# An LRU in-projection in three passes on split values, with its heads written out, and filler matmuls in TensorE's waits

## The reference

```
proj = x @ w_in                      # (288, 2048) @ (2048, 4096)
gate_br, u = split(proj, 2)
uc = causal depthwise conv of u (4 taps) + bias
r  = sigmoid(uc @ w_a + b_a);  ig = sigmoid(uc @ w_x + b_x)     # per head, 8 heads of 256
a  = exp(-8 * r * softplus(-lambda));  b = sqrt(1 - a^2) * ig * uc
h  = scan over time of  h = a*h + b
out = (h * gelu(gate_br)) @ w_out
x  = layer_norm(alpha * x + out)
x  = layer_norm(alpha * x + moe(x))  # 4 groups x 4 experts, routed, 2 experts per token
```

## Time and profile before

| | |
|---|---|
| median of 3 runs | 1817.91 us (1817.19 to 1818.08) |
| profiled execution, its own time | 1817.13 us |
| its span, first to last instruction | 1815.1 us |
| mean granted TensorE clock | 0.953 |
| PE busy | 1659.0 us (91%), 7572 instructions |
| PEld / DVE / ACT busy | 1200.1 / 1313.6 / 1070.6 us |
| LRU heads, first in-projection product to the end of the last head's line 841 | 26.70 to 306.70 us |
| out-projection | 324.02 to 427.46 us |
| time in the chain of waits on line 830 / 841 | 14% / 2% of the span |

### The profile page before, as it was taken

The page is one execution under the profiler, slowest core; times in us unless marked ns, Lnnn a source line. Parts: engine busy times, 40 slices in busy tenths (PEclk is TensorE's granted clock), DMA queues, the critical chain, the costliest instruction groups (busy, mean ns, idle before and its releaser), DMA issues.

```text
span 1815.1 us, 20866 instructions
## 1 busy us (share of the span) xinstructions
PE 1659.0 (91%) x7572; PEld 1200.1 (66%) x7572; DVE 1313.6 (72%) x1658; ACT 1070.6 (59%) x1223; POOL 45.0 (2%) x34
## 2 busy tenths in 40 slices
PE   6999997897799999999999958869999999999995
PEld 5777775895576666766666636556665675665664
DVE  1333334654678998998998856567899899899887
ACT  1132224333657787787787842355877777777774
POOL 0000000000000000000000000000001001000100
PEclk9999999899889999999999977888999999999998
DMA  9443436252479999999999962266998999998990
GB/s 285 141 153 113 150 127 208 93 177 101 156 280 325 388 366 329 400 357 344 378 360 341 372 220 93 98 226 249 369 368 333 339 389 332 344 385 330 337 381 14
DMA packets 146405, 487.90 MB, mean 269 GB/s; under 512 B 5324, under 2 KB 59276, under 8 KB 126892
## 3 DMA queue, kind: packets, MB, share of 16 engines
q1 hardware_dynamic: 141328, 463.75, 69.7%
q0 software_dynamic: 2464, 13.37, 2.5%
q10 hardware_dynamic: 2522, 9.59, 1.6%
HBM read 476.15 MB, written 14.47 MB: 270 GB/s over the span
## 4 chain that ended last, share of the span: by engine, by line
PE 77%; DVE 12%; issue 4%; ACT 3%; DMA 2%; ACTq 1%; DVEq 0%; POOL 0%; POOLq 0%
PE ps L997 17%; PE ps L999 16%; PE ps L998 16%; PE ps L830 14%; DVE ring_lo L1415 6%; PE ps L859 2%; PE ps L861 2%; PE ps L860 2%; PE ps L1042 2%; PE ps L841 2%; PE ps L915 1%; DVE xtok L1373 1%; DVE zstat L1377 1%; DMA xtok<-x_rows,src_now 1%; PE ps L923 1%
## 5 line engine op out<-in xcount | busy, mean ns | idle before, releaser
L1415 DVE TENSOR_TENSOR ring_lo<-ring,whi 128x1024 fp32r<-128x1024 f32 x768 | 922.1, 1221 | 115.7 <-ACT whi L703 108.3
L703 ACT ACTIVATE whi<-ring 128x1024 fp32r<-128x1024 f32 x768 | 806.2, 1060 | 256.2 <-PE ps L999 249.2
L997 PE MATMUL ps<-whi,operands 128*96 128x512 f32 x1536 | 625.0, 407 | 35.3 <-issue 17.6
L999 PE MATMUL ps<-ring_lo,operands 128*96 128x512 f32 x1536 | 610.7, 398 | 0.0
L998 PE MATMUL ps<-whi,operands 128*96 128x512 f32 x1536 | 608.9, 396 | 0.0
L997 PEld LDWEIGHTS ps<-whi,operands 128*96 128x96 f32 x1536 | 250.4, 163 | 169.4 <-DVE ring_lo L1415 40.4
L999 PEld LDWEIGHTS ps<-ring_lo,operands 128*96 128x96 f32 x1536 | 251.1, 163 | 112.4 <-issue 0.2
L998 PEld LDWEIGHTS ps<-whi,operands 128*96 128x96 f32 x1536 | 252.7, 165 | 100.1 <-issue 0.8
L830 PE MATMUL ps<-xT,ring 128*128 128x288 f32 x1024 | 249.7, 406 | 0.7 <-ACT mark L571 0.7
L830 PEld LDWEIGHTS ps<-xT,ring 128*128 128x128 f32 x1024 | 194.4, 190 | 54.6 <-ACT mark L571 0.8
L859 PE MATMUL ps<-operands,whi 128*128 128x288 f32 x256 | 76.7, 300 | 17.3 <-DVE ylo L1205 17.3
(11 more groups left out here) (263 smaller groups left out, 1039.9 us busy)
## 6 DMA issues: line engine op xcount, KB each, us to landing
ring<-in_moe_w_gate_up SPq DMA_DIRECT2D x128, 2048.0 KB, 9.1
ring<-in_moe_w_down SPq DMA_DIRECT2D x64, 2048.0 KB, 9.9
ring<-in_lru_w_in SPq DMA_DIRECT2D x16, 2048.0 KB, 9.6
ring<-in_lru_w_out SPq DMA_DIRECT2D x8, 2048.0 KB, 8.5
x_rows<-xtok ACTq DMA_DIRECT2D x4, 1024.0 KB, 3.9
ring<-in_pool_w SPq DMA_DIRECT2D x4, 1024.0 KB, 6.4
xtok<-in_x_prompt SPq DMA_DIRECT2D x2, 1024.0 KB, 9.2
ring<-in_lru_w_a SPq DMA_DIRECT2D x8, 256.0 KB, 5.4
```

Source lines behind the costliest of these rows:

```text
L703: eng.activation(whi[:, i % NPART, :], ring_at(n)[:, at * PART:(at + 1) * PART], ACT.Copy)\
L997: mm(o, hi, whi[:, i % NPART, cols], start=start, stop=False)
L999: last = mm(o, hi, lo_at(base + i // PARTS_CHUNK, i % PARTS_CHUNK)[:, cols], start=False, stop=stop)
L1415: TT_(lo_at(n, at), ring_at(n)[:, at * PART:(at + 1) * PART], whi[:, i % NPART, :].bitcast(F32), ALU.subtract).then_inc(lo_ready, 1)
```

## The change

The in-projection works on split values as the out-projection does. `x` is split into `yhi` and into 16 blocks of `xlo`, which lie in the unused part of the two ring slots that hold `w_a` and `w_x`. The eight heads are written out on SP, ACT, PE and DVE instead of looped. The first four parts of the next head (for the last head, of the out-projection) are split inside the head before. `SelfOrder` counts per head (14 links instead of 28 per turn). `chunks_done` now counts once per head, so its later thresholds are smaller. In addition PE runs 12, 8 and 10 matmuls whose results nobody reads, at three kinds of place: 12 at the start of each mixture of experts, 8 before the first window of each, and 10 at the end of layer 0.

```diff
+PARTS_HEAD = 2 * PARTS_CHUNK
+PARTS_LRU = HEADS * PARTS_HEAD
+XLO_SPLIT = 10
...
+        def xlo_block(k):
+            slot, at = (SLOT0 + 2) % NSLOT if k < XLO_SPLIT else (SLOT0 + 5) % NSLOT, 1024 + (k % XLO_SPLIT) * T
+            return ring_lo[:, slot, at:at + T]
...
```

On SP:

```diff
+            def lru_slot_free(n):
+                if n % 3 < 2:
+                    eng.wait_ge(parts_used, NPART + (n // 3) * PARTS_HEAD + (n % 3 + 1) * PARTS_CHUNK)
+                else:
+                    eng.wait_ge(chunks_done, n // 3 + 1)
...
             for i in range(N_OUT):
                 n = C_OUT + i
                 if i < NSLOT:
-                    eng.wait_ge(chunks_done, n - NSLOT + 1)
+                    lru_slot_free(n - NSLOT)
+                    if i == 2:
+                        eng.wait_ge(parts_used, NPART + PARTS_LRU)
...
```

On ACT:

```diff
+            def high_part(p):
+                n, at = ((p // PARTS_HEAD) * 3 + (p % PARTS_HEAD) // PARTS_CHUNK if p < PARTS_LRU else
+                         C_OUT + (p - PARTS_LRU) // PARTS_CHUNK), p % PARTS_CHUNK
+                if at == 0:
+                    eng.wait_ge(ring_ready[slot_of(n)], ready_at(n))
+                eng.wait_ge(parts_used, p + 1)
+                eng.activation(whi[:, p % NPART, :], ring_at(n)[:, at * PART:(at + 1) * PART], ACT.Copy)\
+                   .then_inc(hi_ready, 1)
+
+            eng.wait_ge(tr_act[0], 6)
+            eng.wait_ge(tr_dve[0], 6)
+            for q in range(4):
+                eng.activation(yhi[:, 4 * q:4 * q + 4, :], xT[:, 4 * q:4 * q + 4, :], ACT.Copy).then_inc(xs_hi, 1)
+                high_part(q)
             eng.wait_ge(derived, 1)
             eng.activation(sp[1][:, :], sp[0][:, :], ACT.Exp, scale=-1.0).then_inc(lam_exp, 1)
             eng.activation(mark[0:1, 30:31], tiny[0:1, 0:1], ACT.Copy).then_inc(u_copied, 2)
...
+            for h in range(HEADS):
+                for p in range(4, 8):
+                    high_part(h * PARTS_HEAD + p)
+                eng.wait_ge(parts_used, NPART + h * PARTS_HEAD + PARTS_CHUNK)
+...
+                for p in range(8, 12):
+                    high_part(h * PARTS_HEAD + p)
+                eng.wait_ge(parts_used, NPART + (h + 1) * PARTS_HEAD)
+...
-            for part in range(PARTS_OUT):
...
+            eng.wait_ge(head_done, HEADS + 1)
+            for k in range(KD):
+                eng.activation(yhi[:, k, :], yT[:, k, :], ACT.Copy).then_inc(yhi_ready, 1)
+            for p in range(PARTS_LRU + NPART, PARTS_LRU + PARTS_OUT):
+                high_part(p)
...
```

On PE:

```diff
+            for h in range(HEADS):
+                for j in range(2):
+                    if j == 1:
+                        eng.wait_ge(gelu_done, h + 1)
+                    else:
+                        eng.wait_ge(u_copied, 2 * h + 2)
+                    for q in range(PARTS_CHUNK):
+                        p = h * PARTS_HEAD + j * PARTS_CHUNK + q
+                        if h == 0 and j == 0:
+                            eng.wait_ge(xs_lo, q + 1)
+                        eng.wait_ge(lo_ready, p + 1)
+                        for k in range(4 * q, 4 * q + 4):
+                            for b in range(2):
...
+                                mm(o, hi, yhi[:, k, :], start=(k == 0), stop=False)
+                                mm(o, hi, xlo_block(k), start=False, stop=False)
+                                last = mm(o, lo, yhi[:, k, :], start=False, stop=(k == KD - 1))
+                        last.then_inc(parts_used, 1)
+...
+            def stay_awake(n):
+                for _ in range(n):
+                    mm(ps[:, 2, 0:T], onesd[:, :], prmT[:, 0:T], start=True, stop=True)
+
             def moe(l):
+                stay_awake(12)
...
                 eng.wait_ge(tr_act[1 + l], 12)
+                if l == 0:
+                    eng.wait_ge(cstT_ready, 1)
+                stay_awake(8)
                 eng.wait_ge(rows_in[l], 16)
...
                 if l == 0:
                     pe_extra.append(eng.snap(n_win - NG))
+                    eng.wait_ge(z_done[0], eng.snap(n_win * 4 + 4))
+                    eng.wait_ge(rows_out[0], eng.snap(n_win * 16))
+                    stay_awake(10)
                     eng.wait_ge(back_in, 48)
...
```

On DVE:

```diff
+            def low_part(p):
+...
+                eng.wait_ge(hi_ready, p + 1)
+                TT_(lo_at(n, at), ring_at(n)[:, at * PART:(at + 1) * PART],
+                    whi[:, p % NPART, :].bitcast(F32), ALU.subtract).then_inc(lo_ready, 1)
+
+            for q in range(4):
+                eng.wait_ge(xs_hi, q + 1)
+                for k in range(4 * q, 4 * q + 4):
+                    ins = TT_(xlo_block(k), xT[:, k, :], yhi[:, k, :].bitcast(F32), ALU.subtract)
+                ins.then_inc(xs_lo, 1)
+                low_part(q)
...
+            for h in range(HEADS):
+                for p in range(4 if h == 0 else 5, 8):
+                    low_part(h * PARTS_HEAD + p)
+...
+                for p in range(8, 12):
+                    low_part(h * PARTS_HEAD + p)
+...
+                if h < HEADS - 1:
+                    low_part(h * PARTS_HEAD + 12)
+...
-            for part in range(PARTS_OUT):
-                n, at = C_OUT + part // PARTS_CHUNK, part % PARTS_CHUNK
-                if part == NPART:
...
+            for k in range(KD):
+                eng.wait_ge(yhi_ready, k + 1)
+                TT_(ylo[:, k, :], yT[:, k, :], yhi[:, k, :].bitcast(F32), ALU.subtract).then_inc(ylo_ready, 1)
+            for part in range(NPART, PARTS_OUT):
```

More of the change, by code:

```diff
@@ L90, in parts_base @@
 def parts_base(l):
[L92 removed]
+    return PARTS_LRU + PARTS_OUT + l * NG * PARTS_WIN
 def slot_of(n):
@@ new lines, in _ @@
+            for h in range(HEADS):
+                for j in range(2):
+                    n = 3 * h + j
+                    if j == 1:
[8 more added lines that the diff above has]
+                        for k in range(4 * q, 4 * q + 4):
+                            for b in range(2):
+                                at = (k % 4) * 256 + b * 128
+                                hi, lo = whi[:, p % NPART, at:at + 128], lo_at(n, q)[:, at:at + 128]
+                                o = ps[:, 2 * j + b, 0:T]
+                                mm(o, hi, yhi[:, k, :], start=(k == 0), stop=False)
+                                mm(o, hi, xlo_block(k), start=False, stop=False)
+                                last = mm(o, lo, yhi[:, k, :], start=False, stop=(k == KD - 1))
+                        last.then_inc(parts_used, 1)
+                n = 3 * h + 2
+                eng.wait_ge(ring_ready[slot_of(n)], ready_at(n))
+                eng.wait_ge(uc_ready, h + 1)
+                eng.wait_ge(ri_read, h + 1)
+                wv = ring_at(n)[:, 0:1024].rearrange("p (a k j) -> p a k j", a=2, k=2)
+                for a in range(2):
+                    for b in range(2):
+                        for k in range(2):
+                            last = mm(ps[:, 4 + 2 * a + b, 0:TG], wv[:, a, k, b * 128:(b + 1) * 128], UC[:, k, :],
+                                      start=(k == 0), stop=(k == 1))
+                last.then_inc(chunks_done, 1)
@@ L849, in _ @@
                 for q in range(PARTS_CHUNK):
-                    part = i * PARTS_CHUNK + q
+                    part = PARTS_LRU + i * PARTS_CHUNK + q
                     if i == 0:
@@ L1198, in _ @@
                 TS_(slot_iota[:, w * W:(w + 1) * W], iota_f[:, 0:W], float(w * W), None, ALU.add)
[L1199 to L1205 removed]
+            for k in range(KD):
+                eng.wait_ge(yhi_ready, k + 1)
+                TT_(ylo[:, k, :], yT[:, k, :], yhi[:, k, :].bitcast(F32), ALU.subtract).then_inc(ylo_ready, 1)
+            for part in range(NPART, PARTS_OUT):
                 if part >= PARTS_CHUNK + NPART and (part - NPART) % PARTS_CHUNK == 0:
                     out_add((part - NPART) // PARTS_CHUNK - 1)
[L1208 to L1210 removed]
+                low_part(PARTS_LRU + part)
             for i in range((PARTS_OUT - 1 - NPART) // PARTS_CHUNK, N_OUT):
```

223 lines of the change are left out of this document (81 added, 142 removed).

## The result

| | before | after |
|---|---|---|
| median of 4 runs each, on one chip | 1817.55 us (1814.25 to 1818.08) | 1775.12 us (1773.60 to 1777.10) |
| ratio of the runs | | 0.9771, 95% interval 0.9760 to 0.9782 |
| profiled execution, its own time / its span | 1817.13 / 1815.1 us | 1773.60 / 1771.8 us |
| mean granted TensorE clock | 0.953 | 0.961 |
| first in-projection product | 26.70 us | 32.92 us |

What follows compares the result with a forecast made beforehand. PE alone was taken to bound the LRU, ACT and DVE hidden. Passes -44.4, start +9.8, end -4.2 give -38.8; with fillers -3.7, -42.5 us: 1775.4 us against the median, range 1766 to 1794.

Steps and rivals of the forecast that it cites:

- The passes: LRU in-projection: three matmuls per product at 0.1327 us each make a head 29.4 us, 44.4 us less for eight.
- Rival (d): In-projection passes spaced by columns alone, 0.120 us each: 19.5 us less, 1756 us; chance 0.03.
- The parts in time: Inside each LRU head, ACT and DVE deliver split parts before PE needs them, thinnest slack 1.9 us; cost nothing.
- Rival (a): Split chain late at the first gate part, seven heads each wait 2.5 us: +17.5, 1793 us; chance 0.13.
- rival (c): Split chain so late that the clock falls every head; a pause costs its length plus 1.5 us; 1835 us; chance 0.04.
- The start: Before PE's first product, ACT's split copies of x delay the mark 8.3 us, plus 1.5 us at half clock: +9.8.
- The end of the LRU: Four subtractions move inside the last head, so the out-projection starts 17.1 us after the last gate part, not 21.3: -4.2.
- writing out the loop: Writing out the loop over heads removes only register work that hides beside PE: nothing.
- The fillers: Unread PE matmuls at three kinds of place in the mixture of experts: -3.7 us together, between -10 and +2.
- the transposes at the end of layer 0: Ten fillers before them: 10 us instead of 13.8 if the clock holds; -5.8 at best, -2.5 taken.
- The toss of the first window of layer 0: Eight fillers leave PE 3.5 us of rest before the experts; if the clock holds, up to 3 us, 1 taken.
- Rival (b): Fillers give nothing or run over while the LRU does as said: 1779 us; chance 0.12.

Runs made afterwards that it cites:

- Experiment 5: Changed kernel with three extra reciprocals on DVE ahead of the subtraction of part 12 (the next head's first gate part); 1808.09 us, one execution.
- experiment 4: Changed kernel with one extra reciprocal on DVE ahead of the subtraction of part 12 (the next head's first gate part); 1774.29 us, one execution.
- experiment 3: Changed kernel with ACT's exp and its two marks moved ahead of the split of x; 1767.89 us, ratio to before 0.9728.
- experiment 7: Kernel before with the heads written out instead of looped on all four engines, nothing else changed; 1815.52 us, ratio to before 0.9990.
- experiment 1: Changed kernel without any of its filler matmuls; 1777.22 us, ratio to before 0.9777.
- experiment 2: Kernel before with the filler matmuls alone added; 1814.12 us, ratio to before 0.9983.
- 8: Changed kernel with 14 (layer 0) and 18 (layer 1) fillers instead of 8 before the first windows; 1768.82 us, ratio to before 0.9740.
- 10: Kernel of experiment 3 plus 8 fillers before the first in-projection part, 20 before the out-projection, and index writes moved behind `ylo`; 1765.82 us, ratio to before 0.9714.
- 11: Kernel of experiment 10 plus 14 and 18 fillers instead of 8 before the layers' first windows; 1761.69 us, ratio to before 0.9689.
- after again: The changed kernel run once more, unedited, on the same chip as the experiments; 1774.15 us, ratio to before 0.9761.
- 6: Changed kernel with the in-projection's second and third passes on 144 of 288 columns; 1767.65 us, one execution.
- experiment 9: Changed kernel with a float32 filler of 128 columns ahead of each of 16 transpose blocks at layer 0's end; 1783.05 us, ratio to before 0.9812.

## Why the prediction was right, step by step

**The passes** (-44.4 us). The head came out at 29.44 us as forecast, 5.53 us less, 44.2 in all. The spacing from the out-projection's rows carried over to 0.1329 us against 0.1327. Rival (d) is out. The Trainium skill's gap for a single warm matmul (TensorE: Matmul & The Clock Gate, Back-to-back issue gap), an estimate of 122.5 ns for 288 columns by N / 2.4 + 2.5, is 10 ns short of these back-to-back products here too.

**The parts in time** (0). Part 12's subtraction ended 14.35 us after the last gate part, in the head that ends at 119.7 us, against a forecast of 14.8, and its slack was 2.4 us against 1.9:

```profile
132.82 1.23 DVE L1155 TENSOR_TENSOR ring_lo<-ring,whi 128x1024 fp32r<-128x1024 f32 x1
```

Experiment 5 measured the same slack from the other side, 2.5 us, and experiment 4 that it can be spent for nothing. Rival (a) did not happen, but it was 2.5 us away: at 3.1 us too late it takes 33.8 of the 42.4 us. That also bears out the pricing in rival (c), the pause plus 1.5 us (here 1.7 on average, though the first pause cost only 0.3 more than its length). No transfer of `w_in` was waited for.

**The start** (+9.8). PE's first product stood 0.42 us behind the last copy of x before (26.28 to 26.70) and 8.77 us behind it after (24.15 to 32.92): 8.35 us later, forecast 8.3. The absolute time, 32.9 instead of 35.0, is off because the inputs landed 2.1 us earlier. The low clock lasted to 38 us, 5.1 us and not the 3.0 that I took from 324 to 327 us: 2.5 us at half speed, less the 0.3 that the first head of before had lost too (31.30 against 31.04), so 2.3 in place of 1.5. Term as measured: +10.7. The prediction took ACT's order as given; experiment 3 shows that 4.6 of the 8.35 us of delay were not the price of the split.

**The end of the LRU** (-4.2). The out-projection started 16.35 us after the last gate part, forecast 17.1; `head_done` came at 14.0 instead of 14.7. The term is -4.9, and `ylo` was the last thing late, as said.

These are -44.2 + 10.7 - 4.9 = -38.4 us against -38.8; the 2.1 us of earlier inputs make up the landmark's -40.65 within rounding. The prediction put writing out the loop at nothing. If the earlier inputs come with it, as the profiles and the 2.1 us of experiment 7 suggest, that term was mis-sized; the LRU without fillers took off 40.3 us by the medians (experiment 1), as -38.4 and -2.1 would have it. This stays open, as said at experiment 7.

**The fillers** (-3.7). Measured 3.1 us on the new kernel and 3.4 on the old. The sum was right and its parts were not. I gave 2.5 us to the transposes at the end of layer 0; against the kernel without fillers they gained 0.6 and the pooling products behind them 1.2. The clock was up when they began and was lost some 1.1 us into them, as the bound with "may not hold it up" had it, and their 13.20 us lie near the 13.8 of "if they don't work". The toss of the first window of layer 0 fell on the wrong side: PE rested 3.51 us, as forecast (3.5), and the next products ran at 0.59, a gain of 0.2 us and not 1. Of the 3.1 us the profiles of after and experiment 1 name about 2.6 (0.2, 1.8 and 0.6 us in layer 1, which I had at nothing), of which the 1.2 us of the pooling group may be chance. The rest is not placed: between the profiles of before and after themselves, only 1.3 us appear from the transposes at the end of layer 0 to the first ones of layer 1 (1198.21 - 1085.78 against 1154.92 - 1043.80). Rival (b), no gain or a loss from the fillers, is out by experiment 2.

**What the profile of before had beside that.** Its products at 542 to 546 us ran at a granted clock of 0.57 after an idle time of 2.44 us; the same place of after has an idle time of 2.45 us and the clock at 1.00. Windows of before:

```profile
542.00:546.00 4.00, 4.00 (x12) 2.65 (x11) 1.23 (x1) 2.06 (x2) 0.00 (x0) 0.57 0.82 334
```

and of after:

```profile
500.00:504.00 4.00, 3.52 (x16) 2.50 (x17) 2.25 (x3) 1.57 (x2) 0.00 (x0) 1.00 1.02 391
504.00:508.00 4.00, 4.00 (x21) 2.88 (x20) 3.43 (x4) 3.00 (x4) 0.00 (x0) 1.00 0.47 147
```

Experiment 7 has the dip too (0.57 at 538 to 542), and so have experiments 4, 8, 10 and 11 behind the same pause of 2.43 to 2.44 us; after again and experiments 1, 2, 3, 5, 6 and 9 don't. So after again repeats after, but the dip goes neither with the new LRU nor with the fillers. About 1.6 us of the 43.3 between the two profiled spans is this, a pause that sometimes costs clock and sometimes doesn't, and not a step of the change.

**How much of it was luck.** The mechanism was right: the passes, the slack, the delay at the start and the shorter end are each within 1 us of their term. That the sum came within 0.3 us of the median is luck in part: the start cost 0.9 us more than forecast and the end gave 0.7 more, the fillers gave 0.6 less and in other places than forecast, and 2.1 us of earlier inputs stood in no term.

## What to carry to other kernels

Where PE is the chain and its products are regular, the spacing of the same shapes elsewhere in the trace prices a rewrite to a per cent; what needs laying out by hand is the one part whose operand passes through two other engines, and its slack. Put the instruction that releases the bound engine ahead of work that it doesn't need: the order of two groups on ACT was worth 4.6 us here by the profiles and 6.3 by the medians, more than all the fillers of the change. Fill a wait up to its end: a filler that leaves 3.5 us of rest bought 0.2 us; lengthened to leave 0.5 us, in both layers, it bought 4 to 6 us in two pairs of kernels (8 against after, 11 against 10).

## What the runs showed of the hardware that was not expected

- With passes of 288, 144 and 144 columns the granted clock stayed at 0.50 for some 47 us while PE showed as busy 100%, and rose in the first float32 products; with three passes of 288 columns it rose after 5.1 us. A busy share of 100% stood beside either level.
- The clock was at 1.00 when the transposes at the end of layer 0 began, fell within 1.1 us (after) and stayed at 0.50 until they ended, in experiment 9 without any idle time of PE from their start on. Whether the transposes or the wait of 2.3 us before them brought it down is open.
- Pauses of one length had two prices: 3.1 us cost 3.4 in the first head of experiment 5 and 4.85 in the next; 2.44 us before the products at 540 us was followed by a lower clock in before and in five other kernels, and 2.45 us at the same place by none in after and in seven others.
- Halving the columns of a pass saved only 16% of it (0.133 to about 0.111 us, if the full pass beside it kept its time).
